# A transformer pair on one core: the latent attention's key norm from sums of four heads in one bank, spread by row groups

## What is computed

```
k_nope = (ckv @ w_uk).reshape(B, S, MLA_HEADS, MLA_NOPE)
v = (ckv @ w_uv).reshape(B, S, MLA_HEADS, MLA_DV)
k = jnp.concatenate([k_nope, jnp.broadcast_to(k_rope[:, :, None, :], ...)], axis=-1)
q = rms_norm(q, q_norm_w)
k = rms_norm(k, k_norm_w)
k = jnp.concatenate([k[..., :MLA_NOPE], apply_rope(k[..., MLA_NOPE:], pos)], axis=-1)
```

```
kk = (k * k_k).reshape(B, S, H, N).astype(jnp.float32)
kk = kk / jnp.maximum(jnp.linalg.norm(kk, axis=-1, keepdims=True), 1e-12)
```

## Time and profile before

| what | value |
|---|---|
| median of 3 runs | 1988.12 us (1987.95 to 1988.39) |
| the profiled execution, its own time | 1986.86 us |
| its span | 1985.1 us |
| granted TensorE clock over the span | 0.991 |
| TensorE busy (PE) | 1929.6 us, 97% |
| VectorE, ScalarE, GpSimd busy | 903.7, 810.8, 966.4 us |

### The profile page before, as it was taken

One profiled execution on the slowest core, in us unless ns is written; L12 is line 12 of the kernel. 1 busy time (PEld: TensorE's weight loads), 2 busy tenths in 40 slices (PEclk: granted clock), 3 DMA queues, 4 the chain that ended last, 5 costly groups with the idle time before them and its releaser, 6 DMA issues.

```text
span 1985.1 us, 26416 instructions
## 1 busy us (share of the span) xinstructions
PE 1929.6 (97%) x10306; PEld 1567.3 (79%) x10306; DVE 903.7 (46%) x1473; ACT 810.8 (41%) x1067; POOL 966.4 (49%) x742
## 2 busy tenths in 40 slices
PE   6999999989999999999999999999999999999997
PEld 3787888867788878888888678878877888888886
DVE  2678659964431333222102885369945521112101
ACT  4568342365552333232223763243337543232221
POOL 3637335643144545655665580033542556554662
PEclk9999999999999999999999998999999999999999
DMA  7312045431112322222234320034221322323222
GB/s 292 107 64 81 27 175 212 174 108 43 44 66 105 137 79 103 99 93 106 85 107 138 127 64 23 12 112 111 102 85 44 128 100 92 106 85 106 105 90 82
DMA packets 30827, 199.40 MB, mean 100 GB/s; under 512 B 5488, under 2 KB 7664, under 8 KB 9712
## 3 DMA queue, kind: packets, MB, share of 16 engines
q1 hardware_dynamic: 30704, 197.72, 28.1%
HBM read 188.79 MB, written 4.19 MB: 97 GB/s over the span
## 4 chain that ended last, share of the span: by engine, by line
PE 85%; DVE 6%; ACT 4%; POOL 3%; DMA 1%; issue 1%; SPq 0%; DVEq 0%; POOLq 0%; ACTq 0%
PE ps L465 23%; PE ps L467 22%; PE ps L466 22%; PE ps L541 2%; POOL WL L2748 1%; PE ps L483 1%; PE ps L484 1%; PE ps L947 1%; PE ps L934 1%; PE ps L571 1%; PE ps L506 1%; DVE ar L2090 1%; ACT WH L1435 1%; PE ps L681 1%; DMA ar<-ada_dram 1%
## 5 line engine op out<-in xcount | busy, mean ns | idle before, releaser
L2748 POOL TENSOR_TENSOR WL<-raw,WH 128x512 fp32r<-128x512 f32 x588 | 784.6, 1334 | 862.2 <-ACT WH L1435 819.7
L465 PE MATMUL ps<-hH,WH 128*128 128x512 f32 x1560 | 618.6, 397 | 8.6 <-ACT ar L1728 5.5
L467 PE MATMUL ps<-hH,WL 128*128 128x512 f32 x1560 | 608.4, 390 | 0.0
L466 PE MATMUL ps<-arR,WH 128*128 128x512 f32 x1352 | 526.0, 389 | 0.0
L1435 ACT CAST WH<-raw 128x2048 fp32r<-128x2048 f32 x147 | 280.9, 1911 | 465.8 <-DMA raw<-panels_dram 464.4
L465 PEld LDWEIGHTS ps<-hH,WH 128*128 128x128 f32 x1560 | 293.3, 188 | 82.1 <-issue 11.4
L467 PEld LDWEIGHTS ps<-hH,WL 128*128 128x128 f32 x1560 | 293.2, 188 | 62.3
L466 PE MATMUL ps<-xL,WH 128*128 128x512 f32 x792 | 309.5, 391 | 0.0
L466 PEld LDWEIGHTS ps<-arR,WH 128*128 128x128 f32 x1352 | 253.8, 188 | 53.1 <-issue 0.5
L465 PE MATMUL ps<-arR,WH 128*128 128x512 f32 x584 | 228.0, 390 | 0.0
L467 PE MATMUL ps<-arR,WL 128*128 128x512 f32 x584 | 227.2, 389 | 0.0
(11 more groups left out here) (395 smaller groups left out, 2266.2 us busy)
## 6 DMA issues: line engine op xcount, KB each, us to landing
raw<-panels_dram SPq DMA_DIRECT2D x145, 1024.0 KB, 4.9
ar<-ada_dram SPq DMA_DIRECT2D x12, 2048.0 KB, 11.1
xT<-xT_dram SPq DMA_DIRECT2D x2, 2048.0 KB, 8.7
out_dram<-xT SPq DMA_DIRECT2D x8, 512.0 KB, 2.8
ar<-ar SPq DMA_DIRECT2D x12, 256.0 KB, 7.4
xT<-out_dram SPq DMA_DIRECT2D x1, 2048.0 KB, 10.8
wide<-wide_dram SPq DMA_DIRECT2D x1, 1024.0 KB, 4.9
ar<-ar SPq DMA_DIRECT2D x8, 128.0 KB, 3.7
```

Of the source, the lines that this page charges most:

```text
L465: mm(out, lhs[0], rhs[0], start=first, stop=False)
L466: mm(out, lhs[0], rhs[1], start=False, stop=False)
L467: return mm(out, lhs[1], rhs[0], start=False, stop=final)
L2748: ins = tt(WL[:, n % SLOTS, c], raw[:, n % SLOTS, c], WH[:, n % SLOTS, c].bitcast(F32), ALU.subtract)
```

## The change

The sums of four heads go side by side into one bank: 32 columns of ones each, so that head q fills rows 32q to 32q+31 (`four_sums`). ScalarE makes one factor tile for four heads. TensorE spreads each head's factor over 128 rows again, from the 32 rows of its group by a matrix whose first row in 32 is one (`spread`), into a bank for each head, which VectorE reads in place of the tile. RS_K is two tiles, neither of them a rotation table. The second group's sums stand between `gate_dn0` 0 and 1, its spread behind `gate_dn0` 1. POOL's squares of heads 4 to 7 wait for the first sums as a whole. The constants grow by a 128x128 matrix.

```diff
@@ -91,7 +91,7 @@
 
 
 CONST_128 = ["ident", "ones", "top64", "low64", "same64", "head_sums", "utri", "neg_after", "strict64",
-             "incl64"]
+             "incl64", "first_of32"]
 
 
 def constants():
@@ -109,6 +109,7 @@
     m["neg_after"] = np.where(j > c, NEG, 0)
     m["strict64"] = same & (j < c)
     m["incl64"] = same & (j <= c)
+    m["first_of32"] = j % 32 == 0
     sq = np.stack([np.asarray(m[k], np.float32) for k in CONST_128], 1)
     wide = np.zeros((6, P, S), np.float32)
     q, k = j, c
@@ -408,7 +409,7 @@
             return sm4[:, which, t, lo:lo + n]
 
         SQUARES, RW_SQUARES = (19, UNIT_COLUMNS), (24, 24)
-        RS_K, QR_SQUARE, KSQ = (15, 48, 51, 52), (10, 15, 48, EXTRA), (14, 49, 10, EXTRA)
+        RS_K, QR_SQUARE, KSQ = (15, 48), (10, 15, 48, EXTRA), (14, 49, 10, EXTRA)
         KRW_SWAP, QR_SWAP, INDEX_SWAP, AQ_SWAP, AK_SWAP = 14, 44, 7, 12, 35
         Q_LOG, Q_SCALE = 0, 1
 
@@ -541,6 +542,20 @@
                     ins = mm(pst(name, i), sel[k] if isinstance(sel, list) else const(sel), sq,
                              start=(k == 0), stop=(k == len(squares) - 1))
                 end(ins)
+
+            def four_sums(out, sel, tiles, squared, n0, start=True, stop=True):
+
+                for q in range(HALF):
+                    pe.wait_ge(squared, n0 + q + 1)
+                    ins = mm(out[32 * q:32 * q + 32, :], sel, tile(tiles[q]), start=start, stop=stop)
+                return ins
+
+            def spread(name, g, src, sel, banks=ALL_BANKS):
+
+                for q in range(HALF):
+                    b = slice(32 * q, 32 * q + 32)
+                    begin(name, HALF * g + q, banks)
+                    end(mm(pst(name, HALF * g + q), const(sel)[b, :], src[b, :], start=True, stop=True))
 
             def halves(qt):
 
@@ -909,6 +924,17 @@
                 for t in range(NT):
                     ins = mm(pst("qss_turn")[:, t * H:(t + 1) * H], tile(MV + 7)[:, t * P:(t + 1) * P], const("head_sums")[:, 0:H], start=True, stop=True)
                 end(ins)
+
+                def latent_key_sums(g):
+
+                    begin("kss", g)
+                    end(four_sums(pst("kss", g), const("ones")[:, 0:32], KSQ, sem("k_sq"), HALF * g))
+
+                def latent_key_spread(g):
+
+                    pe.wait_ge(sem("k_rstd"), g + 1)
+                    spread("kss_unit", g, tile(RS_K[g]), "first_of32")
+
                 w = panel("ukv", 1, D)
                 for i in range(8):
                     t, half = i // 2, i % 2
@@ -918,9 +944,9 @@
                     end(ins)
                     if i == 7:
                         done_with("ukv", 1)
-                    if i % 4 == 3:
-                        for h in range(i - 3, i + 1):
-                            column_sums("kss", h, [tile(KSQ[h % 4])], [(sem("k_sq"), h + 1)])
+                    if i == 3:
+                        latent_key_sums(0)
+                latent_key_spread(0)
 
                 emptied(pe, "mv", 7)
 
@@ -930,7 +956,7 @@
                     for j in range(2):
                         h = 2 * p + j
                         if qt == 0:
-                            pe.wait_ge(sem("k_scaled"), h + 1)
+                            emptied(pe, "kss_unit", h)
                         mm(outs[j][:, k], tile(QN + h)[:, q], tile(KN + h)[:, k], start=True, stop=False)
                     ins = [None, None]
                     for c in halves(qt):
@@ -948,7 +974,10 @@
                                      turned[j][:, kt * P:(kt + 1) * P], start=(kt == 0), stop=(kt == qt))
                     return ins
 
-                project("gate_dn0", h_mix, 2)
+                project("gate_dn0", h_mix, 1)
+                latent_key_sums(1)
+                project("gate_dn0", h_mix, 1, i0=1)
+                latent_key_spread(1)
                 attention("mla", UNITS, score, value, (12, 13, 14, 11), (15, 48),
                           chain(woven("gate_dn0", h_mix, 2, 2), woven("gate_mla0", h_mix, 4), woven("gate_dn1", h_mix, 2)))
                 for fb in range(2):
@@ -1726,9 +1755,9 @@
                     for i in range(4 * g, 4 * g + 4):
                         filled(act, "mv", i)
                         link(nc.scalar.copy(tile(MV + i), pst("mv", i)), *read("mv", i))
-                    if g == 0:
-                        act.wait_ge(sem("q_roped"), 4)
-                    rstds("kss", range(4 * g, 4 * g + 4), RS_K, 1.0 / 192, sem("k_rstd"), sem("k_scaled"))
+                    filled(act, "kss", g)
+                    link(af(tile(RS_K[g]), pst("kss", g), ACT.Ln, bias=col("eps"), scale=1.0 / 192), *read("kss", g))
+                    link(af(tile(RS_K[g]), tile(RS_K[g]), ACT.Exp, scale=-0.5), sem("k_rstd"), g + 1)
                 for m in range(2):
                     filled(act, "gate_dn0", m)
                     link(af(tile(GATE["gate_dn0"][m]), pst("gate_dn0", m), ACT.Sigmoid), *read("gate_dn0", m))
@@ -2406,11 +2435,11 @@
                 for h in range(HALF, H):
                     key_squares(h)
                 for h in range(H):
-                    dve.wait_ge(sem("k_rstd"), h + 1)
-                    rs = tile(RS_K[h % 4])
+                    filled(dve, "kss_unit", h)
+                    rs = pst("kss_unit", h)
                     b = slice(64 * (h % 2), 64 * (h % 2) + 64)
                     link(stt(tile(KN + h), tile(KN + h), weights, rs, ALU.mult, ALU.mult))
-                    link(tt(tile(KR + h // 2)[b, :], tile(KRW)[b, :], rs[b, :], ALU.mult), sem("k_scaled"), h + 1)
+                    link(tt(tile(KR + h // 2)[b, :], tile(KRW)[b, :], rs[b, :], ALU.mult), *read("kss_unit", h))
                 def mla_between(u):
                     if u in (7, 11, 15):
                         for h in (u // 2 - 3, u // 2 - 2):
@@ -2848,7 +2877,7 @@
                     if i == H + 2:
                         pool.wait_ge(pe_done, last["qss", 0])
                     if i >= H + 4:
-                        pool.wait_ge(pe_done, last["kss", i - H - 4])
+                        pool.wait_ge(pe_done, last["kss", 0])
                     x = tile(QN + i) if i < H else tile(KN + i - H)
                     link(tt(tile(MV + i) if i < H else tile(KSQ[i % 4]), x, x, ALU.mult), sem("nope_sq"), i + 1)
                 add_squares("rms2", 24, "wo")
```

## The result

| | before | changed |
|---|---|---|
| median, 4 runs each | 1988.26 us | 1999.4 us |
| lowest and highest | 1987.95, 1988.86 | 1997.45, 2001.09 |
| profiled execution, span, granted clock | 1986.86, 1985.1, 0.991 | 1997.45, 1995.7, 0.986 |

The account below looks back on a forecast made before the run. TensorE, busy 97% of the span, was taken to bound the kernel. A gain of 5.3 us in the key norm and a loss of 9.5 in block 2 gave +4.2, on the median 1992.3 us; range 1988.5 to 1996.0.

Parts of the forecast that it names:

- a group of sums: Key norm: four heads' sums side by side take 0.93 us; two rounds replace eight sums, 5.0 us less.
- a group of spreads: Key norm: four new spread matmuls run at once in 0.95 us a group, 1.9 us more in all.
- left of the 5.49 us: Key norm: of TensorE's 5.49 us standstill until ScalarE's copy of `mv` 7, 1.1 us of wait is left.
- wait for bank 6, until: Before `gate_dn0` 2: TensorE waits 3.5 us until VectorE's scaling frees bank 6 at 453.6.
- wait in front of `rkv` 2: Block 2: `rkv` 2 must wait until VectorE has read `kkn` 3; two waits become one of 10.7 us.
- loss from `kkn` to `rm`: Block 2: shifted banks cost 7.5 us of waiting and 2.0 us of lower clock, 9.5 us in all.
- 3.5 is near the former, and I take full clock: Behind the bank 6 wait: 3.5 us is near the 3.26 us wait with a fast product behind it, so full clock.
- the 5.3 us: First place, the key norm: the first transposes start at 462.2 and not at 467.51, 5.3 us won.
- rival 1: First place: the bank 6 wait lowers the clock, or spreads run one by one; gain 3.3 us, 1994.3 us; chance 0.27.
- so the other engines go back by the same 9.5 us: Block 2: `mix` 7 and ScalarE's tap need `rkv` 2, two CASTs stand behind; other engines move 9.5 us later.
- a gain of 1.7 and a loss of 11: Worse ends: first place, one-by-one spreads and lower clock; second place, lower clock for twice as long.
- Rival 3: Block 2: the wait of `rkv` 2 for VectorE costs nothing, 5.3 us stand alone: 1982.8 us; chance 0.08.

Follow-up runs that it names:

- e8: e3 with the spreads of heads 4 and 5 swapped, so bank 6 is free one head later: 1984.1 us, ratio 0.9981.
- e7: The changed kernel run again with no edit, on another chip: 2000.36 us, ratio 1.0066 to the kernel before.
- e3: The changed kernel with the bank rotation brought back and the second group's spreads in banks 6, 7, 4, 5: 1982.14 us, ratio 0.9966.
- e6: The changed kernel with ScalarE's two CASTs of the rm panel ahead of tap 7: 1996.13 us, ratio 1.0047.
- e1: The changed kernel with the bank rotation brought back, after the second spread, to where it was before the change: 1987.85 us, ratio 0.9989.
- e4: e3 with the second spread moved into the middle of `gate_dn0` 1: 1981.4 us, ratio 0.9958.
- e11: The kernel of e4 again on another chip: 1981.31 us, ratio 0.9957.
- e2: The kernel before with the bank rotation moved on by two after `gate_dn0` 1, nothing else: 2002.44 us, ratio 1.0061.
- e9: e3 with the sums of heads 4 to 7 put back ahead of `gate_dn0` 0: 1987.97 us, ratio 0.9989.

## Why the prediction was right and wrong

**Right, with the measured number.**

| step | forecast | measured |
|---|---|---|
| a group of sums | 0.93 us | 1.0 (427.08 to the next product at 428.07) |
| a group of spreads | 0.95 | 1.07 (448.07 to 449.14) |
| left of the 5.49 us | 1.1 | 0.85 |
| squares done | 441.5 | 440.96 |
| wait for bank 6, until | 3.5, 453.6 | 3.63, 453.91 |
| peaks possible | 455.1 | 455.31 |
| wait in front of `rkv` 2 | 10.7 | 10.72 |
| loss from `kkn` to `rm` | 9.5 | 8.8, 7.5 of waiting and 1.3 of clock |

By the estimate from the Trainium skill's page "TensorE: Matmul & The Clock Gate", section "Measured speedup vs the span model", a group of spreads takes 1.1 us; the row of 1.07 agrees with it and not with my 0.95.

**Wrong, first.** The step was "3.5 is near the former, and I take full clock". The wait came as laid out, and behind it the window reads 0.56. From the first product behind the wait to the first transposes TensorE took 11.4 us (453.91 to 465.30), where I had 8.6. 2.8 of the 5.3 us are gone so, which was rival 1, at 0.27; but rival 1 priced the clock at 2.0 us, and 13 products stood behind the wait at half clock, not ten. I had read 3.26 us with full clock and 5.49 with half as the two sides of a border, from one case each. e8 shows the clock falling behind 2.13 us, the result and e7 show both outcomes at 2.04, and the very wait of 3.26 us of the earlier trace rows went both ways. So did a wait of 2.7 us at 218.7, in front of TensorE's next work: full clock in before and in the result, 0.58 from 218.5 to 222.5 us in e3. The window of the 3.26 us before, which takes in the end of the wait:

```profile
729.00:734.00 5.00, 3.35 (x15) 2.81 (x16) 4.79 (x7) 2.89 (x4) 0.00 (x0) 1.00 0.00 0
```

Changed, where the wait ends at 728.41:

```profile
729.00:734.00 5.00, 5.00 (x17) 3.95 (x16) 4.75 (x8) 2.38 (x5) 0.00 (x0) 0.66 0.00 0
```

So the length of a wait alone doesn't tell. With evidence that thin, the fallen clock belonged in the forecast and the full one among the rivals.

**Wrong, second.** The step was "so the other engines go back by the same 9.5 us", priced at nothing. They do go back by that, but TensorE goes back by less. Its two waits became one, so the 1.81 us that it used to stand in front of `rm` took up part of the delay: `rm` came 7.7 us later. ScalarE's CASTs hang on the tap of `rkv` 2, which has no such slack: 1148.10 to 1157.69, 9.6 us later, and POOL's work, in order behind them, as much (the splitting at 1181.64 was at 1172.04). The panel had been 0.18 us late before; it is now late by 9.6 - 7.7 = 1.9 us more, the 2.04 us of the row. e6 takes this wait away by the place of the CASTs alone. +1.9 us were missing from the sum, and up to 1.5 more where the clock falls behind it.

**Not in the sum.** 1.5 us lie in the chain of block 2, from the wait of 1.15 us to that of 1.03 us, where the window from 1190 to 1260 has a clock of 0.85, and before 0.88:

```profile
1190.00:1260.00 70.00, 67.61 (x892) 0.88 0.05 17
```

This stretch is 75.68 us long in the result's profile and 74.18 before. But e7, the same changed kernel, has 74.17, and e1, whose block 2 is as before the change, 75.66. This differs between executions of one program and isn't the change's. The 1.2 us behind the wait of 3.26 us weren't in the sum either: the prediction used that wait as an example of full clock and put nothing on it.

**The sum and the range.** -5.3 and +9.5 were measured as -2.5 and +8.8; the rest is +1.2 (clock at the wait of 3.26), +1.9 (panel) and +1.5 (chain; in e7 the 1.5 us lie behind the panel wait instead). "Slower" was not luck: the loss of block 2 outweighs the gain by the mechanism laid out. The miss of 7.1 us (1999.4 against 1992.3) is mostly clock, 2.8, 1.2 and 1.5 us in the profile, and the panel's 1.9. The worse ends of my two terms, a gain of 1.7 and a loss of 11, would have given 1997.4 us (a clock down for twice as long is 7.5 + 4.0 = 11.5 of loss by my own terms, so 1997.9); I stopped at 1996.0, as if clock falls at several places didn't come together. Rival 3, faster, needed block 2 not to wait, and nothing in the changed kernel gave it that; e3 and e4 do, by two small edits.

**Open.** In all eleven profiles with the new key norm (the result, e1, e3 to e11) the clock fell behind the wait of 3.26 us, in the two without it (before, e2) it didn't: from there to `kkn` it is 406.35 to 407.91 us in the eleven and 405.64 in the two. No edit touches that place, and two profiles are too few to call this an effect of the change. What decides whether the clock falls behind such a wait was not found and not tried, so the cause of this part of the error stays open.

## What to carry to other kernels

Where banks are dealt from one rotation, count how many a change takes, and look at every later job with a bank of its own; two small edits (e3) turned 11 us lost into 7 us won. Give the bank that the next job needs first to the value that is read first. And price a wait like those here (2.04 to 3.63 us) at its length, with the slow products behind it, up to 1.7 times as much, as a second outcome; then look for what else stands on another engine behind the job that comes late.

## What was unexpected in the hardware

The same wait of 2.04 us in the same program was followed by full clock in one execution and by half clock in another, and by seven slow products in e2 too. Four waits of 1.13, 0.56, 0.62 and 0.62 us with single matmuls of 32 columns between them (e9) left the clock at 1.00, while one of 2.13 us (e8) did not. A float32 matmul of 32 columns alone took 1.0 us in e9 (441.59 to the next product at 442.57), and four of them into four column groups took 1.0 us together (427.08 to 428.07).
